# Second attentions: order of copies on VectorE and ScalarE, and the gate pieces' pattern on TensorE

## The chip, the cores and the metric

The kernel runs on one core of one Trainium2 chip. The metric is the device time of one execution in microseconds (us); the figure for a kernel is the median of its runs. The engines are called as in the profile: PE (TensorE matmul), PEld (TensorE weight load), DVE (VectorE), ACT (ScalarE), POOL (GpSimd), SP (SyncE, which issues the DMAs).

## What is computed

Two blocks follow one another on 1024 tokens of width 1024. The second block projects its input to four branches; two of them are attentions with 4 heads of width 64 each. The change is in the program part that computes these two attentions:

```python
# forgetting attention ("fox")
logits = jnp.einsum('bqhd,bkhd->bhqk', qb, kf) * scale
logits = logits + jnp.moveaxis(cb, 1, 2)[..., None] - c_key[:, :, None, :]
logits = jnp.where(kpos[None, :] <= qpos[:, None], logits, -jnp.inf)
probs = jax.nn.softmax(logits, axis=-1)
return jnp.einsum('bhqk,bkhd->bqhd', probs, vf)
...
# stick-breaking attention ("stick")
log_rest = jnp.where(mask, jax.nn.log_sigmoid(-z), 0.0)
between = lax.cumsum(log_rest, axis=3, reverse=True) - log_rest
weights = jnp.where(mask, jnp.exp(jax.nn.log_sigmoid(z) + between), 0.0)
return jnp.einsum('bhqk,bkhd->bqhd', weights, vf)
...
# behind them
merged = sum(jax.nn.sigmoid(gates[:, :, n]) * (branches[n] @ w_branch[i, n]) for n in range(N_BRANCHES))
```

The product that gives `gates` (1024 tokens by 4096 columns) needs nothing of the attentions. Its matmuls are dealt out in small pieces between the matmuls of the other branches.

## The kernel before

`attention_branches` runs 64 steps, each one tile of 128 queries of one head: 32 stick and 32 fox. Steps 0 to 3 are stick, steps 4 to 59 are fox (even) and stick (odd) by turns, steps 60 to 63 are fox. A query tile t (0 to 7) sees (t+1)*128 keys, so a step's instructions are 128 to 1024 columns wide. A fox step and the stick step behind it have the same tile. From step 4 on the tiles go 4, 5, 6, 7, 0, 1, 2, 3 and so on: three and a half rounds of a wide stretch (tiles 4 to 7, eight steps) and a narrow one (tiles 0 to 3, eight steps).

Every engine has its own list of instructions, written by a loop over the steps i, and they meet by semaphores alone. Nothing is reordered by a scheduler: an instruction that waits holds all that stands behind it on its engine.

- PE, step i: `score(i)` (L2096 and the mask L2099), gate pieces (L1061; a piece is three matmuls of 512 columns), in even steps `outputs(i - 4)` (L2123: the outputs of steps i-4 and i-3), then `transposes(i - 2)` (L2110). For seven steps (`values`) the transposes of a head's values (L2076) are put in, ahead of the gate pieces and behind the outputs.
- ACT, stick step i: Abs, Exp, Ln of the scores (L2170 to L2172), then the copy of the transposed weights of step i-2 from PSUM to `probT` (L2190). Fox step i: the last exponential of the stick step before (L2178), the fox exponential (L2184, it reads the bias `small` that DVE's maximum gives), then the copy of step i-2 (L2190).
- DVE, stick step i: reciprocal and scaling of the fox step before (L2217, L2219), in each fourth step the read-out of a gate half (L1088), then L2234, the scan L2238 and the subtraction L2242, which gives `logits` and frees the score bank. Fox step i: two copies of outputs (L2228), then the maximum (L2248).
- POOL splits the gate weights into a high and a low part (L199, L203: `w_lo`), each time that PE has ended a gate tile of 16 pieces.

`score(i)` of a wide stick step waits until L2242 of the stick step before has read its bank. `transposes(i)` wait for the weights and for the copy of step i-1. `outputs` wait for the copies of both of their steps. `pieces(i)` says how many gate pieces PE takes in step i: 2, but 0 in steps 24 to 27 (`WIDE`) and 4 in steps 64 and 65, 128 in all.

Of the kernel before, what the change touches and what calls it, by code (L numbers as in the profile page):

```python
# [25 lines left out]
ACT = mybir.ActivationFunctionType  # L26
# [3 lines left out]
P = 128  # L30
# [1296 lines left out]
class InputRows:  # L1327
# [15 lines left out]
    def step(self, ins):  # L1343
        self.done += 1
        ins.then_inc(self.row_step, 1)
        self.dve.wait_ge(self.row_step, self.done)
# [369 lines left out]
BR_S5, BR_FOX, BR_RWKV, BR_STICK = 0, 2, 4, 6  # L1716
# [18 lines left out]
def chain(eng, sem):  # L1735

    done = [0]

    def link(ins):
        done[0] += 1  # L1740
        ins.then_inc(sem, 1)
        eng.wait_ge(sem, done[0])
    return link
# [181 lines left out]
def attention_branches(core, io, gates, masks, vecs, ybr):  # L1925
# [4 lines left out]

    LEAD, WIDE = 4, 24
    STICK, FOX = 0, 1
    nc = core.nc
    gates.two = False
# [6 lines left out]
    probT = core.sb("probT2", [P, 2, NQ2, P])  # L1943
# [12 lines left out]
    count = len(steps)  # L1956
# [3 lines left out]
    def stick(i):  # L1960
        return 0 <= i < count and steps[i][0] == STICK

    def fox(i):
        return 0 <= i < count and steps[i][0] == FOX
# [4 lines left out]
    def head(i):  # L1969
        return steps[i][1] // NQ2  # L1970

    def tile(i):

        return (steps[i][1] + (NQ2 // 2 if fox(i) else 0)) % NQ2

    def width(i):
        return (tile(i) + 1) * P

    def pieces(i):


        if i in range(WIDE, WIDE + 4):
            return 0
        return 2 if i < count else 4 if i < count + 2 else 0

    def last_step(kind, hd):
        return steps.index((kind, NQ2 * hd + NQ2 - 1))

    def bank(i):

        return 2 * steps[i][0] + (tile(i) % 2 if tile(i) < 4 else 0)
# [5 lines left out]
    def outputs_until(i):  # L1997

        return 2 * (i // 2) + 2

    def scores(i):
        return core.psum[:, bank(i):2 * steps[i][0] + 2, :].rearrange("p a n -> p (a n)")[:, 0:width(i)]
# [4 lines left out]
    with core.phase("at_f_in", "at_qk_s0", "at_qk_s1", "at_qk_f0", "at_qk_f1", "at_v_s", "at_v_f", "at_s5_in",  # L2007
# [141 lines left out]
        @block.scalar  # L2149
        def _(act):  # L2150
            step = chain(act, abs_step)
            nc.scalar.preload_act_table_set("natural_log_exp_and_others")

            def save_values(kind, hd):
                act.wait_ge(vT_done, value_order.index((kind, hd)) + 1)
                if hd >= 2:
                    act.wait_ge(out_done, outputs_until(last_step(kind, hd - 2)))
                nc.scalar.activation(v[:, kind, hd % 2, :], core.psum[:, 4, :], ACT.Copy).then_inc(v_saved, 1)
            act.wait_ge(f_dve, 1)
            step(nc.scalar.activation(e, f[:], ACT.Abs))  # L2160
            step(nc.scalar.activation(e, e, ACT.Exp, scale=-1.0))
            nc.scalar.activation(e, e, ACT.Ln, bias=1.0).then_inc(f_act, 1)
            save_values(STICK, 0)
            for i in range(count + 2):
                if stick(i):
                    sp = soft[:, number(i) % 2, 0:width(i)]
                    act.wait_ge(scores_done, i + 1)
                    if number(i) >= 2:
                        act.wait_ge(stick_free, number(i) - 1)
                    step(nc.scalar.activation(sp, scores(i), ACT.Abs))  # L2170
                    step(nc.scalar.activation(sp, sp, ACT.Exp, scale=-1.0))
                    nc.scalar.activation(sp, sp, ACT.Ln, bias=1.0).then_inc(ln_ready, 1)  # L2172
                if i in values:
                    save_values(*values[i])
                if stick(i - 1):
                    lg = prob[:, (i - 1) % 3, 0:width(i - 1)]
                    act.wait_ge(stick_free, number(i - 1) + 1)
                    nc.scalar.activation(lg, lg, ACT.Exp).then_inc(stick_prob, 1)  # L2178
                if fox(i):
                    b = slice(number(i) % 2, number(i) % 2 + 1)  # L2180
                    act.wait_ge(fox_bias, number(i) + 1)
                    if i >= 3:
                        act.wait_ge(probT_done, i - 2)
                    nc.scalar.activation(prob[:, i % 3, 0:width(i)], scores(i), ACT.Exp, bias=nmx[:, b],  # L2184
                                         accum_out=total[:, b]).then_inc(fox_exp, 1)
                if i >= 2:
                    act.wait_ge(probT_done, i - 1)
                    if i >= 4:
                        act.wait_ge(out_done, outputs_until(i - 4))
                    nc.scalar.activation(probT[:, i % 2].rearrange("p t n -> p (t n)")[:, 0:width(i - 2)],  # L2190
                                         core.psum[:, 4:6, :].rearrange("p a n -> p (a n)")[:, 0:width(i - 2)],
                                         ACT.Copy).then_inc(probT_saved, 1)

        @block.vector
        def _(dve):
            link = chain(dve, arg_step)
            dve.wait_ge(f_in, 32)
            nc.vector.tensor_scalar(f[:], f[:], fbias[:, 0:1], None, ALU.add).then_inc(f_dve, 1)
            dve.wait_ge(f_act, 1)
            nc.vector.tensor_scalar(f[:], f[:], 0.0, None, ALU.min).then_inc(f_dve, 1)  # L2200
            dve.wait_ge(f_dve, 2)
            nc.vector.tensor_tensor(e, e, f[:], ALU.subtract).then_inc(f_dve, 1)
            dve.wait_ge(f_dve, 3)
            dve.wait_ge(ones_set, 1)
            nc.vector.tensor_tensor_scan(f[:], one[0:HEADS2].broadcast_to([HEADS2, T2]), e, 0.0, ALU.mult, ALU.add).then_inc(f_dve, 1)
            gates.two = True
            gates.vector(dve)
            gates.vector(dve)
            gates.two = False
            for i in range(count + 3):  # L2210
                if fox(i - 1):
                    n = number(i - 1)
                    b, weights = slice(n % 2, n % 2 + 1), prob[:, (i - 1) % 3, 0:width(i - 1)]
                    dve.wait_ge(fox_exp, n + 1)
                    if n >= 1:
                        dve.wait_ge(fox_prob, n)
                    nc.vector.reciprocal(inv[:, b], total[:, b]).then_inc(fox_inv, 1)  # L2217
                    dve.wait_ge(fox_inv, n + 1)
                    nc.vector.tensor_scalar(weights, weights, inv[:, b], None, ALU.mult).then_inc(fox_prob, 1)  # L2219
                if pieces(i) and sum(pieces(n) for n in range(i + 1)) % KT == 0:  # L2220
                    gates.vector(dve)
                if i >= 4 and i % 2 == 0:
                    dve.wait_ge(out_done, i - 2)
                    for n in range(2):
                        x = i - 4 + n
                        hd, j = head(x), tile(x)
                        row = (BR_FOX if fox(x) else BR_STICK) + hd // 2
                        nc.vector.tensor_copy(ybr[64 * (hd % 2):64 * (hd % 2) + 64, row, j * P:(j + 1) * P],  # L2228
                                              core.psum[64 * n:64 * n + 64, 6, 0:P]).then_inc(out_saved, 1)
                if stick(i):  # L2230
                    n, w = number(i), width(i)
                    lg, sp = prob[:, i % 3, 0:w], soft[:, n % 2, 0:w]
                    dve.wait_ge(ln_ready, n + 1)
                    link(nc.vector.scalar_tensor_tensor(out=sp, in0=scores(i), scalar=0.0, in1=sp,  # L2234
                                                        op0=ALU.max, op1=ALU.add))
                    if n >= 1:
                        dve.wait_ge(stick_free, n)
                    link(nc.vector.tensor_tensor_scan(rest[:, 0:w][:, ::-1], one[:].broadcast_to([P, w]), sp[:, ::-1], 0.0,  # L2238
                                                      ALU.mult, ALU.add))
                    if i >= 3:  # L2240
                        dve.wait_ge(probT_done, i - 2)
                    nc.vector.tensor_tensor(lg, scores(i), rest[:, 0:w], ALU.subtract).then_inc(stick_free, 1)  # L2242
                if fox(i):
                    n = number(i)
                    dve.wait_ge(scores_done, i + 1)
                    if n >= 2:
                        dve.wait_ge(fox_exp, n - 1)
                    nc.vector.reduce_max(nmx[:, n % 2:n % 2 + 1], scores(i), AX, negate=True).then_inc(fox_bias, 1)  # L2248


def rwkv_branch(core, io, gates, masks, vecs, ybr):
# [2351 lines left out]
```

## Time and profile before

| | us |
|---|---|
| median of 3 runs (lowest to highest) | 3297.46 (3296.94 to 3301.5) |
| the profiled execution's own time | 3294.64 |
| its span | 3292.9 |
| PE busy in the span | 3123.1 (95%) |
| DVE busy | 2155.1 (65%) |
| ACT busy | 1076.1 (33%) |
| POOL busy | 974.3 (30%) |
| first score to the last output copy of this part | 284.96 |

The part with the change stands from 2043.09 to 2328.05 us of the span. Behind it the program goes on only when all engines have come to the part's end: the next part begins by loading the gates again from memory and multiplying the branches. PE is busy nearly all of the time, so what counts is where PE waits, and at which of its two clock levels (1.2 and 2.4 GHz) it runs; the windows show this as a mean granted clock, where 1.00 is 2.4 GHz and 0.50 is 1.2 GHz.

### The profile page before, as it was taken

What the parts mean: (1) busy time and instruction counts of PE and PEld (TensorE: products, weight loads), DVE (VectorE), ACT (ScalarE), POOL (GpSimd) and SP (SyncE); (2) the same over time, 40 slices, a digit from 0 to 9 for tenths busy, and PEclk for the clock granted to TensorE, in tenths of its full rate; (3) what the DMA queues carried; (4) which work ended last, traced back from release to release, by engine and by line L of the source; (5) the groups of instructions that cost most, each with busy time, mean ns of one, the idle gap of its engine ahead of it and who ended that gap; (6) DMA issues with size and microseconds to landing.
All of it is one profiled execution on the core that took longest, in us unless ns stands there. A gap on an engine that the chain in (4) does not pass through costs nothing. (4 is left out here: it accounts for less than half of the span.)

```text
span 3292.9 us, 42007 instructions
## 1 busy us (share of the span) xinstructions
PE 3123.1 (95%) x16974; PEld 2675.3 (81%) x16974; DVE 2155.1 (65%) x2576; ACT 1076.1 (33%) x1559; POOL 974.3 (30%) x642
## 2 busy tenths in 40 slices
PE   7999999999899899999999999988899999999997
PEld 7997888999788897878868987666677886888875
DVE  4535664444466638898466546656767666897788
ACT  2013432101243413221122222555423643344644
POOL 2320001333000034552224322101241443554575
PEclk9999999999999999999989999989999999999998
DMA  3120000211100013333330004111461444455443
GB/s 138 45 61 14 22 1 19 74 46 50 35 30 1 1 39 132 122 128 104 105 137 33 1 12 129 51 42 46 153 217 61 147 157 153 147 170 179 146 158 122
DMA packets 114352, 282.13 MB, mean 86 GB/s; under 512 B 15298, under 2 KB 21058, under 8 KB 114144
## 3 DMA queue, kind: packets, MB, share of 16 engines
q1 hardware_dynamic: 110848, 274.73, 25.5%
q10 hardware_dynamic: 3312, 4.72, 0.4%
q8 instruction: 135, 2.21, 0.3%
q14 instruction: 57, 0.47, 0.0%
HBM read 237.37 MB, written 41.42 MB: 85 GB/s over the span
## 5 line engine op out<-in xcount | busy, mean ns | idle before, releaser
L4044 PE MATMUL psum<-x,w_hi 128*128 128x512 f32 x2016 | 625.8, 392 | 8.3 <-DVE x L4015 3.2
L199 POOL CAST w_hi<-w_raw 128x1024 fp32r<-128x1024 f32 x98 | 107.6, 1098 | 1620.6 <-PE psum L212 953.7
L4044 PEld LDWEIGHTS psum<-x,w_hi 128*128 128x128 f32 x2016 | 378.5, 188 | 92.9 <-issue 7.0
L4044 PE MATMUL psum<-x,w_lo 128*128 128x512 f32 x1008 | 392.9, 390 | 0.0
L1061 PE MATMUL psum<-h,w_hi 128*128 128x512 f32 x1024 | 331.2, 405 | 20.0 <-PEq L126 8.4
L3929 POOL TENSOR_TENSOR w_lo<-w_sum,w_hi 128x512 fp32r<-128x512 f32 x180 | 250.6, 1399 | 333.9 <-ACT w_hi L3923 333.9
L203 POOL TENSOR_TENSOR w_lo<-w_raw,w_hi 128x1024 fp32r<-128x1024 f32 x98 | 260.5, 2658 | 15.1 <-DVE y L1876 7.3
L1061 PEld LDWEIGHTS psum<-h,w_hi 128*128 128x128 f32 x1024 | 191.6, 193 | 71.9 <-issue 21.0
L4044 PEld LDWEIGHTS psum<-x,w_lo 128*128 128x128 f32 x1008 | 189.6, 188 | 39.7
L212 PE MATMUL psum<-hn_hi,w_hi 128*128 128x348 f32 x864 | 189.4, 328 | 17.2 <-DVE hn_lo L409 15.7
L1061 PE MATMUL psum<-h,w_lo 128*128 128x512 f32 x512 | 203.9, 398 | 0.0
L212 PE MATMUL psum<-hn_lo,w_hi 128*128 128x348 f32 x864 | 185.4, 323 | 0.0
L212 PE MATMUL psum<-hn_hi,w_lo 128*128 128x348 f32 x864 | 185.3, 323 | 0.0
L3923 ACT ACTIVATE w_hi<-w_sum 128x512 fp32r<-128x512 f32 x180 | 112.4, 630 | 208.6 <-DVE w_sum L3911 208.4
L212 PEld LDWEIGHTS psum<-hn_hi,w_hi 128*128 128x128 f32 x864 | 147.6, 190 | 20.2 <-issue 14.1
L1543 ACT ACTIVATE prob<-psum,softmax_small 116x1044 f32<-116x1044 f32 x72 | 81.5, 1132 | 207.3 <-DVE softmax_small L1588 207.3
L212 PEld LDWEIGHTS psum<-hn_lo,w_hi 128*128 128x128 f32 x864 | 147.4, 190 | 0.0
L212 PEld LDWEIGHTS psum<-hn_hi,w_lo 128*128 128x128 f32 x864 | 146.9, 190 | 0.0
L3911 DVE TENSOR_TENSOR w_sum<-w_raw 128x512 f32<-128x512 f32 x121 | 118.9, 986 | 27.9 <-PE psum L4044 21.5
L1511 PE MATMUL psum<-kept_slots,wqk 128*128 128x348 f32 x384 | 121.3, 457 | 5.3 <-PEq L126 3.2
L2696 DVE TENSOR_TENSOR rw_mixed<-rw_mixed,psum 128x512 f32<-128x512 f32 (+1 forms) x96 | 61.0, 642 | 87.7 <-PE psum L2873 86.7
L4077 DVE TENSOR_TENSOR hidden<-hidden,psum 128x1024 f32<-128x1024 f32 x64 | 76.5, 1216 | 63.5 <-ACT hidden L4070 41.9
(498 smaller groups left out, 6904.9 us busy)
## 6 DMA issues: line engine op xcount, KB each, us to landing
w_raw<-in_w_mlp SPq DMA_DIRECT2D x169, 256.0 KB, 2.9
norm_factor<-in_w_mlp SPq DMA_DIRECT2D x87, 256.0 KB, 2.9
w_raw<-in_w_mlp SPq DMA_DIRECT2D x42, 512.0 KB, 3.4
w_raw<-in_w_in SPq DMA_DIRECT2D x36, 512.0 KB, 3.4
w_raw<-in_w_gates SPq DMA_DIRECT2D x32, 512.0 KB, 4.3
gates_kept<-gate_stage SPq DMA_DIRECT2D x64, 256.0 KB, 2.1
gates<-gates_kept SPq DMA_DIRECT2D x32, 512.0 KB, 3.3
w_raw<-in_w_out SPq DMA_DIRECT2D x24, 512.0 KB, 3.5
```

Source lines behind the costliest of these rows:

```text
L199: self.core.nc.gpsimd.tensor_copy(self.hi[:, g % 2], self.raw[:, g % 2]).then_inc(self.hi_done, 1)
L203: self.core.nc.gpsimd.tensor_tensor(self.lo[:, g % 2], self.raw[:, g % 2], self.hi[:, g % 2].bitcast(F32), ALU.subtract) \
L212: last = nc.tensor.matmul(acc[:, c, :], w[:, g % 2, k, :], x(k)[:, c * ch:(c + 1) * ch], start=(k == 0 and part == 0), stop=(k == kt - 1 a ...
L1061: last = nc.tensor.matmul(self.core.psum[:, self.bank(x // KT), :], one[:, g % 2, k, :], other(k)[:, c * CH2:(c + 1) * CH2], start=(k == 0 ...
L1511: last = nc.tensor.matmul(bank(j), wqk[n % 2][:, k0 + k, cols], slots[:, src + k, chunk(c)], start=(k == 0), stop=(k == kt - 1))
L1543: nc.scalar.activation(prob[s % 2].rearrange("p (c n) -> p c n", c=3), scores, ACT.Exp, bias=nmx[:, s % 2:s % 2 + 1], scale=MLA_SCALE, acc ...
L2696: nc.vector.tensor_tensor(both, both, pair_bank(g)[:, first:2], ALU.subtract) \
L3911: self.core.nc.vector.tensor_tensor(self.slot(self.core.weights.sums, j), raw[:, 0:4], raw[:, 4:8], self.SUMS[q]).then_inc(self.w_summed, 1)
L3923: self.core.nc.scalar.activation(self.slot(self.core.weights.hi, j), self.weight_source(j), ACT.Copy) \
L3929: self.core.nc.gpsimd.tensor_tensor(self.slot(w.lo, j), self.weight_source(j), self.slot(w.hi, j).bitcast(F32), ALU.subtract).then_inc(sel ...
L4044: last = self.core.nc.tensor.matmul(out, one[:, k, :], other[:, k, :], start=(group == 0 and k == 0 and part == 0), stop=(group == second ...
L4077: self.core.nc.vector.tensor_tensor(part, part, self.bank_pair(e), op).then_inc(self.added, 1)
```

## The change

Three edits, all in `attention_branches`. On DVE the two output copies move from the middle of the step to its end. On ACT the copy of the transposed weights moves ahead of the fox exponential. On PE the number of gate pieces changes: 1 in even steps and 3 in odd ones up to step 59, steps 24 to 27 included, then 1, 1, 0, 0, 4, 2, 0 in steps 60 to 66; the sum is 128 as before.

```diff
-    LEAD, WIDE = 4, 24
+    LEAD = 4
...
     def pieces(i):
-        if i in range(WIDE, WIDE + 4):
-            return 0
-        return 2 if i < count else 4 if i < count + 2 else 0
+        if i < count - 4:
+            return 3 if i % 2 else 1
+        return (1, 1, 0, 0, 4, 2, 0)[i - count + 4]
...
                     nc.scalar.activation(lg, lg, ACT.Exp).then_inc(stick_prob, 1)
+                if i >= 2:
+                    act.wait_ge(probT_done, i - 1)
+                    if i >= 4:
+                        act.wait_ge(out_done, outputs_until(i - 4))
+                    nc.scalar.activation(probT[:, i % 2].rearrange("p t n -> p (t n)")[:, 0:width(i - 2)],
+                                         core.psum[:, 4:6, :].rearrange("p a n -> p (a n)")[:, 0:width(i - 2)],
+                                         ACT.Copy).then_inc(probT_saved, 1)
                 if fox(i):
...
                                          accum_out=total[:, b]).then_inc(fox_exp, 1)
-                if i >= 2:
-                    act.wait_ge(probT_done, i - 1)
...
                 if pieces(i) and sum(pieces(n) for n in range(i + 1)) % KT == 0:
                     gates.vector(dve)
-                if i >= 4 and i % 2 == 0:
-                    dve.wait_ge(out_done, i - 2)
...
                     nc.vector.reduce_max(nmx[:, n % 2:n % 2 + 1], scores(i), AX, negate=True).then_inc(fox_bias, 1)
+                if i >= 4 and i % 2 == 0:
+                    dve.wait_ge(out_done, i - 2)
+                    for n in range(2):
+                        x = i - 4 + n
...
+                        nc.vector.tensor_copy(ybr[64 * (hd % 2):64 * (hd % 2) + 64, row, j * P:(j + 1) * P],
+                                              core.psum[64 * n:64 * n + 64, 6, 0:P]).then_inc(out_saved, 1)
```

On ACT, at the fox step of tile 7 (widths 1024; the transposed weights that are copied are 896 wide), the list before was

```order
L2178 ACTIVATE logits<-logits 128x896
L2184 ACTIVATE logits,small_149<-psum,small_149 128x1024
L2190 ACTIVATE probT_144<-psum 128x896
L2170 ACTIVATE soft<-psum 128x1024
L2171 ACTIVATE soft<-soft 128x1024
L2172 ACTIVATE soft<-soft 128x1024
L2190 ACTIVATE probT_144<-psum 128x896
```

and it is now (L2190 has become L2183, L2184 has become L2191)

```order
L2178 ACTIVATE logits<-logits 128x896
L2183 ACTIVATE probT_144<-psum 128x896
L2191 ACTIVATE logits,small_149<-psum,small_149 128x1024
L2170 ACTIVATE soft<-psum 128x1024
L2171 ACTIVATE soft<-soft 128x1024
L2172 ACTIVATE soft<-soft 128x1024
L2183 ACTIVATE probT_144<-psum 128x896
```

The first of the two copies has changed places with the fox exponential; the second stays behind Ln.

On PE, steps 24 and 25 (tile 6, in the stretch that had no gate pieces) read before

```order
L2096 MATMUL psum<-keys,queries 128x512
L2096 MATMUL psum<-keys,queries 128x384
L2099 MATMUL psum<-masks_hi 128x128
L2123 MATMUL psum<-probT_144,v_141 64x128 x10
L2110 MATMUL psum<-masks,logits 128x128 x6
L2096 MATMUL psum<-keys,queries 128x512
L2096 MATMUL psum<-keys,queries 128x384
L2099 MATMUL psum<-masks_hi 128x128
L2110 MATMUL psum<-masks,logits 128x128 x6
```

and step 25 now has three pieces between its score and its transposes:

```order
L2096 MATMUL psum<-keys,queries 128x512
L2096 MATMUL psum<-keys,queries 128x384
L2099 MATMUL psum<-masks_hi 128x128
L1061 MATMUL psum<-h_82,w_hi 128x512
L1061 MATMUL psum<-h_84,w_hi 128x512
L1061 MATMUL psum<-h_82,w_lo 128x512
L1061 MATMUL psum<-h_82,w_hi 128x512
L1061 MATMUL psum<-h_84,w_hi 128x512
L1061 MATMUL psum<-h_82,w_lo 128x512
L1061 MATMUL psum<-h_82,w_hi 128x512
L1061 MATMUL psum<-h_84,w_hi 128x512
L1061 MATMUL psum<-h_82,w_lo 128x512
```

Its transposes (L2110) follow behind these. In each other odd step one piece has come in at this place, and in each even step one has gone.

On DVE, from the subtraction of the stick step of tile 6 to the scaling of the fox step of tile 7, the list read before

```order
L2242 TENSOR_TENSOR logits<-psum,rest 128x896
L2228 COPY branches<-psum 64x128 x2
L2248 TENSOR_REDUCE small_149<-psum 128x1
L2217 RECIPROCAL small_149<-small_149 128x1
L2219 TENSOR_SCALAR logits<-logits,small_149 128x1024
```

and now

```order
L2234 TENSOR_TENSOR logits<-psum,rest 128x896
L2240 TENSOR_REDUCE small_149<-psum 128x1
L2247 COPY branches<-psum 64x128 x2
L2217 RECIPROCAL small_149<-small_149 128x1
L2219 TENSOR_SCALAR logits<-logits,small_149 128x1024
```

The maximum stands ahead of the two copies.

## Rows read from the trace of the kernel before

**Rows 1.** Windows: the part cut at the first score of each stretch; last row whole.

```profile
core 0: us, PE busy (x) PEld busy (x) DVE busy (x) ACT busy (x) POOL busy (x), PEclk, DMA share, GB/s
2043.09:2056.96 13.87, 13.40 (x68) 9.68 (x68) 10.13 (x16) 7.78 (x19) 3.76 (x2) 1.00 0.87 226
2056.96:2097.53 40.57, 35.83 (x239) 25.66 (x237) 27.30 (x35) 23.63 (x35) 3.42 (x2) 1.00 0.16 60
2097.53:2125.72 28.19, 26.28 (x155) 18.73 (x156) 17.00 (x36) 13.30 (x33) 3.41 (x2) 0.94 0.25 67
2125.72:2169.55 43.83, 36.04 (x217) 25.95 (x215) 27.73 (x37) 25.00 (x37) 3.40 (x2) 0.84 0.14 37
2169.55:2195.26 25.71, 24.67 (x157) 17.62 (x155) 14.80 (x31) 11.95 (x30) 3.43 (x2) 1.00 0.16 43
2195.26:2239.59 44.33, 38.66 (x231) 27.02 (x231) 26.64 (x35) 23.29 (x34) 3.62 (x2) 0.92 0.21 59
2239.59:2267.27 27.68, 25.54 (x163) 18.33 (x163) 15.83 (x35) 13.95 (x34) 3.42 (x2) 1.00 0.12 39
2267.27:2305.89 38.62, 35.34 (x222) 24.45 (x223) 25.05 (x33) 22.70 (x32) 3.75 (x2) 1.00 0.08 28
2305.89:2328.05 22.16, 18.46 (x123) 13.82 (x121) 9.02 (x24) 6.88 (x15) 0.00 (x0) 1.00 0.06 24
2043.09:2328.05 284.96, 254.21 (x1560) 181.25 (x1560) 173.51 (x274) 148.49 (x263) 28.21 (x16) 0.96 0.19 54
```

**Rows 2.** Waits of PE in the part: us in total, times, longest.

```profile
PE psum L2123 <- ACT probT L2190: 9.2, 10, 2.6
PE psum L2096 <- DVE logits L2242: 9.2, 10, 1.9
PE psum L2110 <- ACT probT L2190: 8.7, 11, 1.9
```

**Rows 3.** Timeline (start, us, what, [wait]), DVE and ACT, fox step of tile 7.

```profile
2227.61 0.59 DVE L2228 COPY branches<-psum 64x128 f32<-64x128 f32 x2
2228.23 1.22 DVE L2248 TENSOR_REDUCE small<-psum 128x1 f32<-128x1024 f32 x1
...
2229.49 1.12 ACT L2184 ACTIVATE logits<-psum,small 128x1024 f32<-128x1024 f32 x1 [0.82 <-DVE small L2248]
...
2230.60 0.91 ACT L2190 ACTIVATE probT<-psum 128x896 f32<-128x896 f32 x1
2231.40 1.02 ACT L2170 ACTIVATE soft<-psum 128x1024 f32<-128x1024 f32 x1
```

**Rows 4.** Groups by shape, ACT, last wide stretch: copies of tiles 5, 4.

```profile
L2190 ACT ACTIVATE probT<-psum 128x768 f32<-128x768 f32 x2 | 1.6, 798 | 0.0
L2190 ACT ACTIVATE probT<-psum 128x640 f32<-128x640 f32 x2 | 1.4, 693 | 0.0
```

**Rows 5.** Timeline, DVE: the subtractions of the last four stick steps.

```profile
2274.54 0.82 DVE L2242 TENSOR_TENSOR logits<-psum,rest 128x640 f32<-128x640 f32 x1
...
2283.75 0.96 DVE L2242 TENSOR_TENSOR logits<-psum,rest 128x768 f32<-128x768 f32 x1
...
2294.29 1.09 DVE L2242 TENSOR_TENSOR logits<-psum,rest 128x896 f32<-128x896 f32 x1
...
2306.04 1.22 DVE L2242 TENSOR_TENSOR logits<-psum,rest 128x1024 f32<-128x1024 f32 x1
```

**Rows 6.** Timeline, POOL's split beside a 768-wide scan, and the same scan alone.

```profile
2138.84 2.37 POOL L203 TENSOR_TENSOR w_lo<-w_raw,w_hi 128x1024 fp32r<-128x1024 f32 x1
...
2140.23 2.59 DVE L2238 TENSOR_TENSOR_SCAN rest<-one,soft 128x768 f32<-128x768 f32 x1
...
2281.96 1.76 DVE L2238 TENSOR_TENSOR_SCAN rest<-one,soft 128x768 f32<-128x768 f32 x1
```

**Rows 7.** Timeline, PE: starts of two gate pieces that follow one another.

```profile
2323.64 0.62 PE L1061 MATMUL psum<-h,w_hi 128*128 128x512 f32 x2
...
2324.33 0.61 PE L1061 MATMUL psum<-h,w_hi 128*128 128x512 f32 x2
```

**Rows 8.** Timeline, DVE: the part's last output copies.

```profile
2327.44 0.61 DVE L2228 COPY branches<-psum 64x128 f32<-64x128 f32 x2 [1.53 <-PE psum L2123]
```

More of the change, by code:

```diff
@@ L2185, in _ @@
                                          accum_out=total[:, b]).then_inc(fox_exp, 1)
-                if i >= 2:
-                    act.wait_ge(probT_done, i - 1)
[L2188 to L2192, printed above, removed]
         @block.vector
@@ L2221, in _ @@
                     gates.vector(dve)
-                if i >= 4 and i % 2 == 0:
-                    dve.wait_ge(out_done, i - 2)
[L2224 to L2229, printed above, removed]
                 if stick(i):
@@ L2248, in _ @@
                     nc.vector.reduce_max(nmx[:, n % 2:n % 2 + 1], scores(i), AX, negate=True).then_inc(fox_bias, 1)
+                if i >= 4 and i % 2 == 0:
+                    dve.wait_ge(out_done, i - 2)
+                    for n in range(2):
+                        x = i - 4 + n
+                        hd, j = head(x), tile(x)
+                        row = (BR_FOX if fox(x) else BR_STICK) + hd // 2
+                        nc.vector.tensor_copy(ybr[64 * (hd % 2):64 * (hd % 2) + 64, row, j * P:(j + 1) * P],
+                                              core.psum[64 * n:64 * n + 64, 6, 0:P]).then_inc(out_saved, 1)
 def rwkv_branch(core, io, gates, masks, vecs, ybr):
```

## The prediction

> **What bounds the kernel now.** I first cut the part into its wide and narrow stretches [rows 1]. PE is busy 254.21 of 284.96 us, so about 31 us are left to waits. A second loss hides in the busy time: the granted clock has a mean of 0.84, 0.92 and 0.94 in three stretches, so PE stood at 1.2 instead of 2.4 GHz for a part of them. One minus the clock, times the stretch, is what it lost: 43.83 * 0.16 = 7.0, 44.33 * 0.08 = 3.5, 28.19 * 0.06 = 1.7, together 12 us, if PE was the bound all along.
>
> Then I asked what PE waits for [rows 2]: 9.2 us for the outputs' and 8.7 us for the transposes' copies on ACT, 9.2 us for the subtraction on DVE that frees the score bank. All three come from one circle: subtraction, fox bias, fox exponential, copy, Abs, Exp, Ln, L2234, scan, next subtraction. The timeline at tile 7 shows its head [rows 3]: behind the subtraction DVE first makes two output copies (0.59 us), then the maximum (1.22 us); ACT waits 0.82 us for it; then come the fox exponential and the 0.91 us copy, and only behind that, at 2231.40, the Abs that the next subtraction hangs on. The circle's length is the distance of the subtractions [rows 5]: ends at 2275.36, 2284.71, 2295.38 and 2307.26, so 9.35, 10.67 and 11.88 us for tiles 5, 6 and 7. A wide stretch has about 36 us of PE work at full clock and lasts 38.6 to 44.3 us [rows 1]: there the circle is the bound. Narrow stretches are nearly filled by PE (24.67 of 25.71 us in the best).
>
> **Copies on ACT and DVE.** No instruction is added or removed. With the copies last on DVE, the maximum comes 0.6 us sooner, and ACT has its copy behind it in the time in which it waited. Neither alone would give all: behind the subtraction ACT now has the stick exponential and the copy (0.91, and the same for the exponential, which is as wide: an estimate), DVE has the maximum (1.22). So the fox exponential starts about where it does now (0.59 + 1.22 us), some 1.8 us behind the subtraction, and the copy behind it is gone. The copy cost 0.80 us there (2230.60 to 2231.40) [rows 3]; at the tiles below, 0.7 and 0.6 us (0.798 and 0.693 less the same overlap) [rows 4]; at the first step of the stretch some 0.5, an estimate by the same fall. That is 2.6 us in each wide stretch. The lower bound is nothing, if something else already closes the circle; the upper is the whole copies, 3.0 us.
>
> What waits anew: the fox exponential now stands behind a copy that needs PE's transposes of that very step. In narrow steps PE is late, but before it the exponential already waited for DVE's copies of outputs that PE makes just ahead of these transposes, plus the maximum. The transposes cost less than those two, so I put this edit at no loss.
>
> DVE's output copies now wait behind the maximum. PE needs them gone only two steps later, and the last ones of the part end it in either order.
>
> **Gate pieces.** A piece takes 0.69 us (2323.64 to 2324.33) [rows 7]. In a pair of steps there are four as before; one has gone from the even to the odd step, which makes the stick transposes and the fox score 0.69 us later, while outputs, fox transposes and the next stick score keep their place. The covers of this are Ln on ACT, which in wide steps ends later than these transposes, and the bias chain, which waits for the subtraction anyway.
>
> Eight pieces (5.5 us) leave the end and go to steps 24 to 27. There, in the fourth row [rows 1], the circle was the bound and PE short of work: 43.83 us, of which the low clock took up to 7.0, with only half the gate pieces to do. I expect this stretch to become like the first wide one, which has the same steps.
>
> Behind the last subtraction (2307.26) the part still takes 2328.05 - 2307.26 = 20.8 us [rows 5, 8], 16 pieces standing from step 60 on. Now there are 8. The pieces of steps 60 and 61 lie beside the circle; 2 + 2 + 2 of steps 62, 63 and 65 leave the path, 6 * 0.69 = 4.1 us, and the copy of step 58, now ahead of a small exponential, may give 0.4 more (an estimate): 4.5 us. Lower bound 2 us, if ACT's copies between them come to the front, upper 5.5.
>
> **POOL's split.** This is the price. A scan beside POOL's low-part subtraction took 2.59 us instead of 1.76 [rows 6]: it came on only as POOL ended (2138.84 + 2.37 = 2141.21, then 1.61 us). The Trainium skill, "GPSIMD Engine Reference", section Specifications, says that GpSimd's memory interfaces are shared with VectorE and contend with instructions of two SBUF inputs; the scan is one, and the trace agrees. POOL splits when PE ends a tile of 16 pieces. Before, these ends fell on steps 7, 15, 23, 35, 43, 51, 59; now on 7, 15, 23, 31, 39, 47, 55: always the stick step of tile 5 or tile 1. At tile 5 the third piece puts POOL 0.69 us later and the shorter circle puts the scan some 0.2 to 0.5 sooner, so the hold grows from 0.83 to about 1.7 us, four times. At tile 1 the scan should be ahead of POOL or have slack. Per stretch it costs 0.9 us more than now in the first two, 1.7 in the last two, which had none at tile 5. Bounds: no hold, or the whole 2.37 each time.
>
> **The sum.** Wide stretches: the first 40.57 - 2.6 + 0.9 = 38.9, gain 1.7. The second, now alike, 39.0: gain 4.8. The third (44.33) has the low clock's 3.5 us in it; with the same steps it comes to 38.9: gain 5.4. The fourth 38.62 - 2.6 + 1.7 = 37.7: gain 0.9. Together 12.8. Narrow stretches, PE's busy time at full clock plus 1.0 us of new waits (an estimate): 26.28 - 1.7 + 1.0 = 25.6 for 28.19, gain 2.6; 25.7 for 25.71, none; 26.5 for 27.68, gain 1.2. Together 3.8. End 4.5. Start: at step 2 PE waits for the first values' copy with one piece less in front, a loss of 0.7. Sum 20.4 us. Against this stand about 2 us of PE waiting behind each tile-7 step and 1 to 2 at tile 5, which can each drop the clock; each drop of the kind seen costs 1.7 us, and I take three: 5.1. Left: 15.3 us.
>
> The rest of the program follows rigidly: the next part begins with all engines at the end of this one.
>
> The profiled execution has 3294.64 us of its own time, 1.74 beyond its span, and lies 2.8 below the median of the runs. It would become 3279.3, the median 3282.
>
> **Rivals.**
> - *The forecast*, gain 9 to 23 us, 3274 to 3288.5: 0.66.
> - *POOL and the clock eat it*: every one of the seven splits holds a scan for the full 2.4 us: four times 0.7 more at tile 5, three times 1.5 at tile 1, and two more drops of 1.7 behind them, 10.7 us. Gain 4.6: 3293. For it: the hold exists [rows 6], and its place moves with the pieces; against it: narrow steps have slack. 0.15. It is the rule of the page above, carried through.
> - *The circle isn't what binds*, and moving the copies gives nothing: then only the end (4.1) and the second wide stretch (43.83 to the first's 40.57, 3.3) gain, less 1.7 for collisions: 5.7 us, 3292. Against it: the fixed distances of 10.67 and 11.88 us. 0.08.
> - *Slower*: three pieces in one block close a circle of their own. If the stick transposes end later than Ln, the copy behind Ln is late, and outputs, fox transposes and, by the new order on ACT, the fox exponential and Abs with it. It decides from the point where the fox score and one piece no longer cover the copy. 0.69 us in each of 28 pairs is 19.3, against 8 still gained by the moved pieces: +11, 3309; in the narrow pairs alone about even. In wide steps Ln is later by over 1 us, which speaks against it. 0.06.
> - *More*: no drops, and no scan of tile 5 held: 20.4 + 4 * 1.7 = 27.2 us, 3270. 0.05.
>
> **How the numbers follow.** About 0.2% (6.6 us) is what can be told from no change. The forecast and *more* are faster, and half of the two small gains: 0.82. The other half is within 0.2%: 0.12. Slower 0.06. The range 3274 to 3292 leaves out *more*, *slower* and half of the small gains, 0.2.
>
> **What would show it.** Right: L2170 starts within 0.1 us of the fox exponential's end; the subtractions of tiles 6 and 7 stand some 0.7 and 0.8 us closer; the four wide stretches are alike within 1.5 us; the part ends some 16 us behind the last subtraction; no stretch has a mean clock under 0.9. Wrong: scans of tile 5 or 1 over 4 us, a wait of the fox exponential for PE's transposes in wide steps, waits of PE for `probT` as long as before (17.9 us in the two groups), or a clock under 0.9 in the second wide stretch.

## The result, and the profile after

The changed kernel takes 3275.01 us (median of 4 runs, 3272.28 to 3275.71), the kernel before 3297.2 us in the same comparison. The ratio is 0.9929, with a 95% interval of 0.9911 to 0.9946: faster by 22 us, where 15 were forecast. The profiled execution has 3275.53 us, its span 3273.7 us.

The windows of the changed kernel, cut at the same scores as [rows 1] (the part now begins at 2045.62):

```profile
2045.62:2059.84 14.22, 12.93 (x65) 9.04 (x65) 9.50 (x16) 7.61 (x19) 3.40 (x2) 1.00 0.90 232
2059.84:2099.95 40.11, 37.10 (x236) 26.91 (x237) 27.91 (x36) 23.78 (x35) 3.40 (x2) 0.96 0.16 56
2099.95:2124.37 24.42, 24.36 (x154) 18.01 (x155) 14.33 (x35) 13.43 (x33) 3.74 (x2) 1.00 0.29 77
2124.37:2163.74 39.37, 36.96 (x241) 26.94 (x239) 28.02 (x35) 23.93 (x35) 3.40 (x2) 0.96 0.17 47
2163.74:2188.19 24.45, 24.39 (x156) 18.00 (x155) 14.52 (x35) 13.44 (x33) 3.73 (x2) 1.00 0.29 76
2188.19:2227.43 39.24, 35.40 (x232) 25.18 (x231) 27.99 (x36) 23.07 (x34) 3.40 (x2) 1.00 0.17 48
2227.43:2253.23 25.80, 25.12 (x162) 18.57 (x163) 14.33 (x35) 14.03 (x34) 3.73 (x2) 1.00 0.13 42
2253.23:2289.78 36.55, 34.30 (x225) 24.67 (x223) 26.53 (x33) 22.34 (x32) 3.40 (x2) 1.00 0.09 30
2289.78:2308.09 18.31, 14.85 (x102) 11.23 (x100) 8.34 (x23) 6.89 (x15) 0.00 (x0) 0.91 0.04 14
2045.62:2308.09 262.47, 245.40 (x1560) 178.55 (x1560) 171.48 (x274) 148.51 (x263) 28.21 (x16) 0.98 0.20 59
```

The part has gone from 284.96 to 262.47 us, 22.5 less. What lies outside it is 3.3 us longer in this one execution (3273.7 - 262.47 = 3011.2 against 3292.9 - 284.96 = 3007.9), though nothing was changed there; over all profiles of this study it lay between 3003 and 3016 us. So in what follows I compare the part's length, which repeats: a second profile of the changed kernel has 262.46 us. The three narrow stretches are filled by PE to 0.1, 0.1 and 0.7 us.

PE's waits in the part, for [rows 2]:

```profile
PE psum L2096 <- DVE logits L2234: 8.4, 7, 1.4
PE psum L2123 <- ACT probT L2183: 4.2, 6, 1.0
PE psum L2110 <- ACT probT L2183: 2.1, 1, 2.1
```

The waits for the two copies are down from 17.9 to 6.3 us; that for the score bank (8.4 of 9.2) has stayed. Why the first fell shows in the timeline of DVE and ACT at the fox step of tile 7, for [rows 3]:

```profile
2216.38 1.21 DVE L2240 TENSOR_REDUCE small<-psum 128x1 f32<-128x1024 f32 x1
2216.50 0.95 ACT L2178 ACTIVATE logits<-logits 128x896 f32<-128x896 f32 x1 [3.64 <-DVE logits L2234]
...
2217.35 0.90 ACT L2183 ACTIVATE probT<-psum 128x896 f32<-128x896 f32 x1
...
2218.15 1.11 ACT L2191 ACTIVATE logits<-psum,small 128x1024 f32<-128x1024 f32 x1
...
2219.24 1.02 ACT L2170 ACTIVATE soft<-psum 128x1024 f32<-128x1024 f32 x1
```

ACT goes from the stick exponential through the copy and the fox exponential to Abs without a pause. The wait of 0.82 us has gone, and Abs begins as the fox exponential ends. Why the bank's wait stayed shows at tile 5, in the timeline of POOL, DVE and PE, for [rows 6]:

```profile
2201.85 2.37 POOL L203 TENSOR_TENSOR w_lo<-w_raw,w_hi 128x1024 fp32r<-128x1024 f32 x1
...
2202.23 3.60 DVE L2230 TENSOR_TENSOR_SCAN rest<-one,soft 128x768 f32<-128x768 f32 x1
...
2206.88 1.77 PE L2096 MATMUL psum<-keys,queries 65*128 65x512 f32 x4 [1.36 <-DVE logits L2234]
```

The scan takes 3.60 us where 1.76 are its own, and PE then waits 1.36 us for the subtraction behind it. That stands in all four rounds (scans of 3.61, 3.61, 3.60 and 3.58 us) and makes 5.5 of the 8.4 us; nearly all the rest are two waits of 1.35 and 1.36 us behind the subtraction of tile 7.

### The profile page after: what moved, and what is told of

Same layout as the page of the kernel before. It is cut to its first block and busy times, and to the rows that moved or that the text cites. A ratio compares the mean times of both kernels' runs of the same rounds, so it can differ in the third digit from the quotient of the medians.

```text
span 3273.7 us, 42007 instructions
## 1 busy us (share of the span) xinstructions
PE 3116.2 (95%) x16974; PEld 2673.1 (82%) x16974; DVE 2155.0 (66%) x2576; ACT 1075.7 (33%) x1559; POOL 975.0 (30%) x642
```

## The experiments

Beside these two, ten kernels ran, one of them the changed kernel once more. The table gives the ratio of runs to those of before on the same chip, and the part's length in the profile (first score to last output copy), which the text compares.

| kernel | ratio (95%) | part, us | to before |
|---|---|---|---|
| before | 1 | 284.96 | |
| changed | 0.9929 (0.9911 to 0.9946) | 262.47 | -22.5 |
| orders_only | 0.9934 (0.9919 to 0.9950) | 271.22 | -13.7 |
| dve_only | 0.9955 (0.9937 to 0.9973) | 269.93 | -15.0 |
| act_only | 0.9958 (0.9942 to 0.9975) | 269.98 | -15.0 |
| pieces_only | 0.9972 (0.9962 to 0.9981) | 277.68 | -7.3 |
| even_pieces | 0.9919 (0.9904 to 0.9934) | 259.13 | -25.8 |
| hole_kept | 0.9961 (0.9948 to 0.9974) | 272.70 | -12.3 |
| split_later | 0.9897 (0.9881 to 0.9914) | 253.01 | -32.0 |
| after_again | 0.9933 (0.9913 to 0.9953) | 262.46 | -22.5 |
| even_split | 0.9913 (0.9895 to 0.9931) | 253.93 | -31.0 |
| even_split_end | 0.9903 (0.9881 to 0.9925) | 252.29 | -32.7 |

**The two reorderings, the gate pieces before's.** `orders_only`:

```diff
-    LEAD = 4
+    LEAD, WIDE = 4, 24
...
-        if i < count - 4:
-            return 3 if i % 2 else 1
-        return (1, 1, 0, 0, 4, 2, 0)[i - count + 4]
+        if i in range(WIDE, WIDE + 4):
+            return 0
+        return 2 if i < count else 4 if i < count + 2 else 0
```

> Both reorderings (copies last on DVE, copy ahead of the fox exponential on ACT), gate pieces as before. Theory (the circle subtraction - exponentials - subtraction is shorter by one copy; the pieces bring the end and the second wide stretch on top): 8 to 12 us below before, part near 274 us, subtractions of tile 6 and 7 near 9.9 and 11.0 us apart, scans of tile 5 held in steps 7 and 23 alone. Rival (all the gain is in where the pieces stand): within 3 us of before.

Measured: 0.9934, the part 271.22 us, 13.7 less. The start is not like the others:

```profile
2039.79:2057.30 17.51, 15.22 (x67) 10.90 (x68) 12.34 (x17) 7.84 (x19) 3.43 (x2) 0.90 0.82 230
```

This stretch lasts 13.2 to 14.2 us in all other profiles; here the clock was at 1.2 GHz for a part of it and a scan of tile 1 (2.51 us) was held by POOL. Only this profile shows it, and its part also began sooner (2039.79) than all others. Whether this comes from the execution or from the lists, one profile can't say. Where it matters I therefore also give the part without its start, from the first score of the first wide stretch on: 271.09 us before, 253.71 here, 17.4 less. In whole times the median is 19.5 us below before's. By any of these the gain is larger than the 8 to 12 us that were expected. The subtractions of tiles 6 and 7 stand 9.65 and 10.83 us apart in the last round, against 10.67 and 11.88 before [rows 5]; 9.9 and 11.0 were expected. The rival falls.

**The pieces alone.** `pieces_only` has the changed `pieces(i)` and both orders of before.

> Only the pieces' pattern changed, both orders as before. Theory: 4 us at the end and 3 to 5 us in the second wide stretch, less 4 times about 1 us of held scans at tile 5 that were not there before and with T of the stick steps later: 3 to 8 us below before; the circle at tile 7 stays at 11.8 us. Rival (pieces are all of the gain): 18 us or more below before. If the two parts simply add up, this and orders_only together give 22 us.

Measured: 0.9972, the part 7.3 us shorter, at the upper end. The circle stays as it was (10.69 and 11.88 us in the last round). But the size is right by luck, for it doesn't lie where it was expected. The end gave 0.6 us instead of 4 and the second wide stretch 1.3 (43.83 to 42.49) instead of 3 to 5, while the three narrow stretches gave 6.1. At the end the clock was low for longer than in any other kernel's (a mean of 0.84):

```profile
2300.34:2321.90 21.56, 16.62 (x102) 12.58 (x100) 8.33 (x23) 6.87 (x15) 0.00 (x0) 0.84 0.03 12
```

Nor do the two halves of the change simply add up. Without the start `orders_only` and `pieces_only` give 17.4 and 7.6 us, together 25.0, and the changed kernel gives 22.8; the totals of 21.0 and 22.5 are near one another only with the long start in them. By stretches:

| gain over before, us | orders_only | pieces_only | changed |
|---|---|---|---|
| four wide stretches | 12.9 | 0.9 | 12.1 |
| three narrow stretches | 4.1 | 6.1 | 6.9 |
| end | 0.4 | 0.6 | 3.9 |

The first narrow stretch counts twice in such a sum: either half alone takes out its low clock (1.7 us) and its held scan of 2.82 us. The end gains only with both.

**Each reordering alone.** `dve_only` has only the output copies at the end of DVE's step, `act_only` only the copy ahead of the fox exponential.

> Only the output copies last on DVE. Theory: the maximum comes 0.6 us sooner behind the subtraction, so ACT's fox exponential may start behind the stick exponential (0.95 us) or the maximum (1.22 us) instead of 1.8 us: the circle at tiles 5 to 7 is shorter by 0.5 us each, 4 to 7 us below before in all. Rival (one order is of no use without the other): within 2 us of before.

> Only the copy ahead of the fox exponential on ACT. Theory: the copy fills ACT's wait for the maximum (0.8 us at tile 7) and its 0.8 us leaves the circle, so nearly the whole gain of the two orders (6 to 10 us below before) comes from this edit alone, and the fox exponential starts where it did, 1.8 us behind the subtraction. Rival: equal shares, or this edit slower because the exponential waits for PE's transposes in narrow steps (up to 3 us above before).

Measured: 15.0 us from the part by either, 0.9955 and 0.9958, and by either a median 12.2 us below before's. Both sizes were expected too small, and the two don't add up in the part: without the start they give 14.3 and 14.9 us, and both together 17.4. (In whole times the two medians would add up to 24.4 us against 19.5; the intervals are too wide to tell.) The same place as above, in `dve_only`:

```profile
2221.26 1.21 DVE L2240 TENSOR_REDUCE small<-psum 128x1 f32<-128x1024 f32 x1
2222.39 0.60 DVE L2247 COPY branches<-psum 64x128 f32<-64x128 f32 x2
...
2222.50 1.11 ACT L2184 ACTIVATE logits<-psum,small 128x1024 f32<-128x1024 f32 x1 [0.18 <-DVE small L2240]
...
2223.61 0.91 ACT L2190 ACTIVATE probT<-psum 128x896 f32<-128x896 f32 x1
2224.41 1.04 ACT L2170 ACTIVATE soft<-psum 128x1024 f32<-128x1024 f32 x1
```

and in `act_only`:

```profile
2220.84 0.59 DVE L2228 COPY branches<-psum 64x128 f32<-64x128 f32 x2
2221.47 1.23 DVE L2248 TENSOR_REDUCE small<-psum 128x1 f32<-128x1024 f32 x1
...
2222.73 1.11 ACT L2191 ACTIVATE logits<-psum,small 128x1024 f32<-128x1024 f32 x1
...
2223.84 1.01 ACT L2170 ACTIVATE soft<-psum 128x1024 f32<-128x1024 f32 x1
```

From the maximum's start to Abs it takes 3.15 us in `dve_only` (the copy of 0.91 us still between). In `act_only` it is 3.00 us from the output copies' start to Abs, and in the changed kernel 2.86 us from the maximum's (2216.38 to 2219.24). Before, it was 3.79 us (2227.61 to 2231.40) [rows 3]. So `dve_only` takes 0.64 us out of the circle, `act_only` 0.79 and both 0.93: two paths run side by side behind the subtraction, DVE's (copies and maximum) and ACT's (stick exponential and copy), and the longer of them counts. With both edits ACT's is the longer; with the output copies still in front, in `act_only`, DVE's is the longer by some 0.1 us.

**The turns of one and three.** `even_pieces` is the changed kernel with

```diff
         if i < count - 4:
-            return 3 if i % 2 else 1
+            return 2
```

> As the changed kernel, but two pieces in every step up to 59 (24 to 27 included) instead of one and three by turns; end as in the changed kernel. Theory A (the turns matter little, the filled steps and the end carry the pieces' part): within 3 us of the changed kernel, 3273 to 3278; POOL's split comes 0.7 us sooner, so scans of tile 5 are held 0.7 us less, up to 3 us for it. Rival B (one and three by turns is what cleared the waits of the stick transposes): 5 us or more above the changed kernel, with waits of L2110 for the copy as before (8.7 us).

Measured: the part 259.13 us, 3.3 less than the changed kernel's; scans of tile 5 take 2.94 to 2.96 us instead of 3.6. The median, 3269.06 us, lies below the 3273 to 3278 that theory A gave, while B had it above the changed kernel's: the turns cost time. PE's waits for the transposes' copies (2.1 us, one of them, at the end) are the same in both, so the turns were not what cleared them. Four times 0.65 us of hold would be 2.6 of the 3.3, but that isn't how it splits. From the subtraction of tile 4 to that of tile 5 it is 0.5 us shorter in three rounds and not in the third, 1.4 in all; from tile 6 to tile 7 it is 1.2 and 0.7 us shorter in the first two rounds, 1.9 in all. There the changed kernel has a low clock and this one has none:

```profile
2061.44:2099.59 38.15, 35.47 (x239) 25.86 (x237) 27.04 (x36) 23.38 (x35) 3.43 (x2) 1.00 0.17 64
2124.19:2162.76 38.57, 35.51 (x241) 26.01 (x239) 27.31 (x36) 23.73 (x34) 3.42 (x2) 1.00 0.18 48
```

PE's wait behind the scan of tile 5 is 0.70 us here instead of 1.37. So the shorter hold came with two low-clock intervals less, and these were the larger part. Between tiles 3 and 4 the even pieces lose 0.4 us in each of three rounds.

**The empty steps.** `hole_kept` is the changed kernel with no pieces in steps 24 to 27 and 2, 2, 2, 2, 4, 4 at the end.

> As the changed kernel, but steps 24 to 27 have no pieces and the end has 2, 2, 2, 2, 4, 4, as before. Theory: the end is longer by 4 us and the second wide stretch hardly shorter (the circle bounds it; clock of 1.2 GHz there for 7 to 10 us): 4 to 7 us above the changed kernel. Rival (the empty steps give back their 5.5 us of PE work): within 2 us of the changed kernel.

Measured: the part 272.70 us, 10.2 more than the changed kernel's. Its windows, for the second wide stretch, the two narrow ones behind it and the end:

```profile
2123.49:2165.34 41.85, 36.71 (x216) 26.69 (x215) 27.95 (x36) 24.85 (x35) 3.39 (x2) 0.82 0.14 38
2165.34:2192.45 27.11, 25.25 (x155) 18.57 (x154) 16.02 (x32) 12.51 (x32) 3.41 (x2) 0.97 0.16 43
...
2231.49:2260.77 29.28, 26.79 (x163) 19.63 (x163) 16.46 (x35) 13.94 (x34) 3.41 (x2) 0.94 0.13 45
...
2297.12:2319.37 22.25, 18.46 (x123) 13.82 (x121) 9.38 (x24) 6.88 (x15) 0.00 (x0) 1.00 0.06 24
```

The end and the second wide stretch are longer by 3.9 and 2.5 us, as expected. The surprise is the narrow stretches, longer by 2.7 and 3.5 us: with eight pieces later, POOL's split falls on tile 3 again, whose scans take 3.34 instead of 1.22 us, and the clock has a mean of 0.97 and 0.94 there. Filling the empty steps was worth more than the two terms I had for it, since it also moved POOL's splits off tile 3.

The kernel before had these held scans too, and all profiles divide by them. In its second and third narrow stretch POOL's split stood beside the scan of tile 3; in the third:

```profile
2263.02 2.39 POOL L203 TENSOR_TENSOR w_lo<-w_raw,w_hi 128x1024 fp32r<-128x1024 f32 x1
...
2264.10 2.39 DVE L2238 TENSOR_TENSOR_SCAN rest<-one,soft 128x512 f32<-128x512 f32 x1
```

and in the changed one the same scan is free:

```profile
2251.14 1.23 DVE L2230 TENSOR_TENSOR_SCAN rest<-one,soft 128x512 f32<-128x512 f32 x1
```

The five profiles in which steps 24 to 27 are empty (before, `orders_only`, `dve_only`, `act_only`, `hole_kept`) have these scans held, and their second and third narrow stretches last 25.6 to 27.1 and 27.3 to 29.3 us. The seven in which they are filled have them free, at 24.3 to 24.8 and 25.8 to 26.0 us. DVE's read-outs of the gates move together with the splits, so no run shows the hold of tile 3 quite apart.

**POOL's split away from the scans.** `split_later` is the changed kernel with a wait in POOL's list, on what DVE's subtraction signals:

```diff
-            gates.gpsimd(pool, 9)
+            for t in range(9):
+                if t >= 2:
+                    pool.wait_ge(stick_free, 4 * t - 2)
+                gates.gpsimd(pool, 1)
```

> As the changed kernel, but each of POOL's weight splits in this part waits until the subtraction of the stick step of tile 5 or 1 is done, so that no scan of tile 5 runs beside it; same work. Theory (the hold of 1.85 us at tile 5 lies on the circle): scans of tile 5 take 1.76 us, PE's wait at the next stick score (1.4 us, four times) goes, 4 to 7 us below the changed kernel, 3268 to 3271. Rival (the hold only takes up slack, the circle of tiles 6 and 7 or PE bounds anyway): within 2 us of the changed kernel.

Measured: 0.9897, the part 253.01 us, 9.5 less than the changed kernel's, more than expected. Its four wide stretches and the last row whole:

```profile
2060.64:2097.55 36.91, 35.21 (x237) 25.78 (x237) 26.64 (x36) 23.67 (x35) 3.42 (x2) 1.00 0.17 61
...
2121.98:2158.83 36.85, 35.30 (x240) 25.81 (x239) 26.75 (x35) 23.70 (x35) 3.42 (x2) 1.00 0.18 51
...
2183.23:2220.67 37.44, 35.04 (x233) 25.17 (x231) 26.75 (x36) 23.11 (x34) 3.42 (x2) 1.00 0.18 50
...
2246.45:2281.19 34.74, 33.93 (x224) 24.62 (x223) 25.31 (x33) 22.32 (x32) 3.43 (x2) 1.00 0.09 31
...
2046.44:2299.45 253.01, 241.02 (x1560) 176.10 (x1560) 171.93 (x274) 147.90 (x263) 27.40 (x16) 0.99 0.21 61
```

The gain is 3.2, 2.5, 1.8 and 1.8 us: the hold of 1.84 us goes straight onto the circle in each round, and in the first two its wait was also followed by a low clock, which has gone with it (0.96 in the changed kernel, 1.00 now). From the subtraction of tile 6 to that of tile 7 it is now 10.82 us in every round. All scans of tile 5 take 1.76 us.

**The changed kernel again, and two combinations.** `even_split` has both even pieces and the later split; `even_split_end` also has the end 2, 4, 1, 1, 0, 0, 0.

> The changed kernel once more, beside the next two on one chip. The part should last 262 to 263 us again and the median lie 20 to 24 us below before; whether the three low-clock intervals (two at tile 7 of the first two rounds, one at the end) come back is open: if they follow from PE's waits they do, if from where the program stands in time they need not.

Measured: 262.46 us, the same three clocks below 1.00 in the same stretches (0.96, 0.96, 0.91), the median 22 us below before's. The part began 3.8 us later than in the other profile and the low-clock intervals came 3.9 us later, so they went with the part. Two executions with one such shift can't show that they always do, so whether they follow from PE's waits alone stays open. They begin between the subtractions of tiles 5 and 6 (at 2079.48 and 2144.33 in the first profile), 1.4 and 1.8 us behind the start of the score that had waited, and not at tile 7, where only their effect shows.

> Two pieces in every step and the split behind the subtraction. With no scan held, the 2.6 us by which two and two were better than one and three (0.65 us less hold, four times) should be gone, so the part lasts 253 us as in split_later, within 1 us: if the advantage of the even pieces was the hold. Rival: the even pieces have an advantage of their own, and the part comes to 250 us.

Measured: 253.93 us, 0.9 more than `split_later`. Without a held scan the even pieces have no advantage left: it was the shorter hold, with the two low clocks that went with it. The rival falls.

> As even_split, with the last eight pieces as 2, 4, 1, 1, 0, 0, 0 in steps 60 to 66 instead of 1, 1, 0, 0, 4, 2, 0. PE's wait of 2.1 us for the copy of step 58 in step 61 takes three of them, and six leave steps 64 and 65. If the end is PE's work (the theory of the prediction, 0.69 us a piece), it gets 2.5 to 4 us shorter: 16.9 to 13 or 14 us behind the last subtraction. If it is the chain of exponential, copy and outputs, under 1 us.

Measured: 252.29 us, 1.6 less. The part ends 15.24 us behind the last subtraction instead of 16.92. That lies between the two theories. Of the six pieces only three moved into PE's wait of 2.1 us, which has gone; two more still stand behind the last subtraction, in steps 62 and 63. But PE now waits 1.09 us for DVE's scaling (at 2298.85), which in `even_split` the pieces of steps 64 and 65 stood in front of; so a part of the end is the chain of exponential, scaling, copy and outputs. Its median (3265.61 us) and `split_later`'s (3263.3 us, on another comparison) can't be told apart. Both beat the changed kernel by the part, 9.5 and 10.2 us. In whole times `even_split_end` has a median 8 us below that of `after_again` (3273.44 us) on the same chip, with intervals that overlap (0.9881 to 0.9925 and 0.9913 to 0.9953); `split_later`'s (0.9881 to 0.9914) touches the changed kernel's (0.9911 to 0.9946) only at its edge.

## Why the forecast was right in direction and too small in size

The mechanism was as forecast: the circle was the bound of the wide stretches, both reorderings shorten it, and POOL's hold at tile 5 takes part of it back. The gain, 22 us, lies at the upper edge of the 9 to 23 that were given. The steps that failed are the clock's term, 5.1 us taken off for what cost 2.0 in the wide stretches, and the narrow stretches' term, 3.8 us for 6.9, where held scans that would go were not counted. Term by term, gains of the changed kernel's windows over [rows 1]:

| term of the sum | forecast, us | measured, us |
|---|---|---|
| wide stretches | 1.7 + 4.8 + 5.4 + 0.9 = 12.8 | 0.5 + 4.5 + 5.1 + 2.1 = 12.1 |
| narrow stretches | 2.6 + 0 + 1.2 = 3.8 | 3.8 + 1.3 + 1.9 = 6.9 |
| end | 4.5 | 3.9 |
| start | -0.7 | -0.4 |
| drops of the clock | -5.1 | in the rows above (2.0 in the wide stretches) |
| sum | 15.3 | 22.5 |

- **The clock's term failed.** "I take three: 5.1". Three low-clock intervals did come, two in wide stretches and one at the end. But between the subtractions of tiles 6 and 7 lie 12.16 and 11.48 us in the first two rounds and 10.82 in the others. The first round and the last:

```profile
2086.55 1.09 DVE L2234 TENSOR_TENSOR logits<-psum,rest 128x896 f32<-128x896 f32 x1
...
2098.58 1.22 DVE L2234 TENSOR_TENSOR logits<-psum,rest 128x1024 f32<-128x1024 f32 x1
```

```profile
2279.24 1.09 DVE L2234 TENSOR_TENSOR logits<-psum,rest 128x896 f32<-128x896 f32 x1
...
2289.93 1.22 DVE L2234 TENSOR_TENSOR logits<-psum,rest 128x1024 f32<-128x1024 f32 x1
```

  So the two cost 1.3 and 0.7 us, not 1.7 each; the distance at tile 6, beside the intervals themselves, is 9.64 us in all four rounds. `split_later`, without these two intervals, has 10.82 in all rounds, which confirms it. The circle was the bound and covered the rest. What the third cost, at the end, no run shows apart.
- **The narrow stretches' term failed.** First, "plus 1.0 us of new waits (an estimate)": there were none, but for a wait of outputs of 0.6 us in the third. Second, the prediction named POOL's splits of before at steps 15, 35 and 51, but not that they hold scans there: one of tile 1 (2.82 us instead of 0.69) and two of tile 3 (2.28 and 2.39 instead of 1.22), one in each narrow stretch. In the changed kernel all three scans are free. It counted what the new places of the splits cost and gave the old ones no value in the narrow stretches; `hole_kept` and the division above point to about 1 us and more in each of the last two.
- **The circle.** Forecast 2.6 us in each wide stretch; the distances at tiles 6 and 7 in the last round went from 10.67 and 11.88 to 9.64 and 10.82 us, 1.0 and 1.1 instead of 0.7 and 0.8. Of this 0.1 us is the step to the fox exponential, which is shorter than I put it (1.77 us from the maximum's start, 1.88 from the output copies' before). The fourth wide stretch, the one with a full clock in both kernels, gained 2.1 us instead of 0.9, and without the hold, in `split_later`, 3.9 instead of 2.6 (with the pieces' pattern changed too). "Neither alone would give all" was right, but each alone gives most of it, 14.3 and 14.9 of 17.4 us without the start.
- **POOL's hold** was forecast at 1.7 us four times, and is 1.85, 1.85, 1.84 and 1.82 us. At tile 1 the scans are free (0.69 us), as forecast. Its price was not: undone, it gives back 9.5 us instead of 6.8, by the two low-clock intervals with it.
- **The end** was "6 * 0.69 = 4.1" plus 0.4; it gave 3.9 (22.16 to 18.31), or 3.85 from the last subtraction on (20.79 to 16.94). The size was near, but the pieces alone gave 0.6 and the orders alone 0.4, so that 4.1 us for the pieces is not shown; in `pieces_only` a longer low clock stood there.
- **The start** lost 0.35 us instead of 0.7.
- Of the rivals, *POOL and the clock eat it* had the hold right and its place too wide: behind the start it stands at tile 5 alone, and of three low clocks the two in wide stretches cost 2.0 us together. *The circle isn't what binds* falls with `orders_only`. *Slower* did not show: PE's transposes wait for a copy only once, at the end, and its outputs 4.2 us in all.
- Of the signs: Abs begins within 0.1 us of the fox exponential's end, the copies' waits fell, the part ends 16.9 us behind the last subtraction and no stretch has a clock under 0.9. But the four wide stretches are alike only to 3.6 us (36.55 to 40.11), since value transposes and low clocks lie unevenly.

## What to carry to other kernels

Where two engines work side by side behind one instruction, an edit on either is worth the difference to the longer path, and two such edits need not add up; test each alone. Moving filler work on one engine moves what it triggers on others: list those triggers (here POOL's splits), what they stand beside now and what they stood beside before, and price both, the hold that comes and the hold that goes. Price a low clock in full only in stretches where that engine is the bound. And compare halves of a change stretch by stretch: `pieces_only` had the expected total from other places than expected.

## What the runs showed of the hardware

- A scan on DVE that starts while POOL's two-input subtraction runs makes almost no headway until that ends: it ends 0.12 to 0.16 us less than its own time behind POOL's end, whatever their overlap. That held in all runs, for scans of 0.69, 0.96, 1.22, 1.76 and 2.29 us (1.61 us behind POOL's end for the one of 1.76, which so took 2.6, 2.95 or 3.6 us). Where a scan of tile 1 in a narrow stretch was first, it kept its time and POOL took 2.70 us instead of 2.37 (at 2110.77, beside a 0.69 us scan at 2110.61). In the kernel before, L2234, with one operand in PSUM, was not slowed beside POOL: 0.96 us at 2139.24 with it, 0.96 us at 2213.40 without.
- Low-clock intervals came again in the same stretches in two executions of one kernel, behind a wait of PE of 1.37 us in two rounds and not behind the same wait (1.36 and 1.37 us) in the other two. Where that wait was 0.70 us or gone (`even_pieces`, `split_later`), none came in the wide stretches. What tells the two rounds from the other two stays open.
